# Expert rows gathered by six rounded products with the token rows split in two halves

## The reference

```python
def _moe(h, router, wg, wu, wd):
    logits = jnp.einsum('btd,de->bte', h.astype(jnp.float32), router.astype(jnp.float32))
    top_v, top_i = lax.top_k(logits, TOP_K)
    probs = jax.nn.softmax(top_v, axis=-1)
    gates = jnp.sum(jax.nn.one_hot(top_i, N_EXPERTS, dtype=jnp.float32) * probs[..., None], axis=-2)
    y = jnp.zeros_like(h)
    for e in range(N_EXPERTS):
        y = y + gates[..., e:e + 1].astype(h.dtype) * _swiglu(h, wg[e], wu[e], wd[e])
    return y
```

## Time and profile before

| | us |
|---|---|
| median of 3 runs | 1846.82 (1846.73 to 1847.57) |
| span of the profiled execution | 1844.9 |
| PE busy | 1671.4 (91%) |
| DVE busy | 1306.2 (71%) |
| ACT busy | 926.0 (50%) |
| GpSimd busy | 248.1 (13%) |

### The profile page before, as it was taken

One profiled execution on the slowest core, in us unless ns is written; L12 is line 12 of the kernel. 1 busy time (PEld: TensorE's weight loads), 2 busy tenths in 40 slices (PEclk: granted clock), 3 DMA queues, 4 the chain that ended last, 5 costly groups with the idle time before them and its releaser, 6 DMA issues.

```text
span 1844.9 us, 31414 instructions
## 1 busy us (share of the span) xinstructions
PE 1671.4 (91%) x11268; PEld 1512.7 (82%) x11268; DVE 1306.2 (71%) x1743; ACT 926.0 (50%) x1229; POOL 248.1 (13%) x132
## 2 busy tenths in 40 slices
PE   6948799989998966789988999999999999999997
PEld 6838786889987965777787979798998979798895
DVE  3798845454401397983536989889898989889896
ACT  4432102244301532211225868777787868778784
POOL 4645310000002553521000000000000000000000
PEclk8968889989999887898988999999999999999999
DMA  6522113265545342112334989989898989989892
GB/s 242 162 69 74 46 69 114 100 214 181 174 128 159 101 132 61 59 49 83 126 126 140 364 300 355 344 308 365 288 365 291 357 310 348 370 285 361 294 360 101
DMA packets 103843, 386.14 MB, mean 209 GB/s; under 512 B 11696, under 2 KB 11728, under 8 KB 103008
## 3 DMA queue, kind: packets, MB, share of 16 engines
q1 hardware_dynamic: 102096, 372.00, 57.1%
q0 software_dynamic: 1680, 13.20, 2.0%
HBM read 377.79 MB, written 7.37 MB: 209 GB/s over the span
## 4 chain that ended last, share of the span: by engine, by line
PE 76%; DVE 18%; ACT 2%; issue 2%; DMA 0%; POOL 0%; SPq 0%; DVEq 0%; ACTq 0%
PE psum L1163 52%; DVE c L816 8%; PE psum L1407 4%; PE psum L1441 3%; DVE qkv L842 2%; PE psum L1198 2%; PE psum L1379 2%; PE psum L1499 2%; PE psum L1381 2%; DVE hT L767 1%; PE psum L1332 1%; PE psum L1362 1%; PE psum L1267 1%; PE psum L1230 1%; PE psum L1206 1%
## 5 line engine op out<-in xcount | busy, mean ns | idle before, releaser
L1098 DVE TENSOR_TENSOR w_lo<-ring,w_hi 128x1024 fp32r<-128x1024 f32 x528 | 644.6, 1224 | 72.0 <-ACT w_hi L711 65.7
L711 ACT ACTIVATE w_hi<-ring 128x1024 fp32r<-128x1024 f32 x528 | 557.7, 1061 | 143.0 <-PE psum L1163 136.0
L1163 PE MATMUL psum<-w_hi,h_hi 128*96 128x256 f32 x1408 | 402.1, 286 | 5.5 <-DVE w_lo L1098 5.5
L1163 PE MATMUL psum<-w_hi,h_lo 128*96 128x256 f32 x1408 | 394.7, 280 | 0.0
L1163 PE MATMUL psum<-w_lo,h_hi 128*96 128x256 f32 x1408 | 393.7, 280 | 0.0
L1163 PE MATMUL psum<-hid_hi,w_hi 128*128 128x264 f32 x1024 | 305.6, 298 | 39.7 <-POOL w_lo L418 30.0
L1163 PE MATMUL psum<-hid_lo,w_hi 128*128 128x264 f32 x1024 | 299.8, 293 | 0.0
L1163 PE MATMUL psum<-hid_hi,w_lo 128*128 128x264 f32 x1024 | 298.9, 292 | 0.0
L1163 PEld LDWEIGHTS psum<-hid_hi,w_hi 128*128 128x128 f32 x1024 | 203.4, 199 | 45.7 <-POOL w_lo L418 30.9
L1163 PEld LDWEIGHTS psum<-w_hi,h_hi 128*96 128x96 f32 x1408 | 228.5, 162 | 8.7 <-DVE w_lo L1098 7.4
L418 POOL TENSOR_TENSOR w_lo<-ring,w_hi 128x1024 fp32r<-128x1024 f32 x68 | 167.3, 2468 | 477.8 <-ACT w_hi L531 477.8
(11 more groups left out here) (280 smaller groups left out, 2000.7 us busy)
## 6 DMA issues: line engine op xcount, KB each, us to landing
ring<-in_w_exp SPq DMA_DIRECT2D x528, 512.0 KB, 5.3
ring<-in_w_mixer SPq DMA_DIRECT2D x112, 512.0 KB, 3.6
ring<-in_w_ffn SPq DMA_DIRECT2D x66, 512.0 KB, 3.5
early<-in_s POOLq DMA_DIRECT2D x2, 2048.0 KB, 8.6
out_ss<-early POOLq DMA_DIRECT2D x2, 2048.0 KB, 6.9
xT<-in_xT SPq DMA_DIRECT2D x1, 1056.0 KB, 5.0
out_yT<-hT POOLq DMA_DIRECT2D x1, 1056.0 KB, 4.2
early<-in_dw_win POOLq DMA_DIRECT2D x2, 496.0 KB, 5.8
```

The source lines that it names most:

```text
L711: A(w_hi[:, (n_split + u) % SPLIT, :], ring[:, u % RING, :, :].rearrange("p k n -> p (k n)"), ACT.Copy).then_inc(hi_done, 1)
L1098: V.tensor_tensor(w_lo[:, (n_split + u) % SPLIT, :], ring[:, u % RING, :, :].rearrange("p k n -> p (k n)"), w_hi[:, (n_split + u) % SPLIT, ...
L1163: last = M(out, lhs[x], rhs[w], start=(start and n == 0), stop=(stop and n == 2))
```

## The change

`h_tok` becomes two tensors of the rounded type: `tok_hi`, which ACT writes at the old place with the same three copies, and `tok_lo`, which DVE writes over `early` with three subtractions of `tok_hi` from the PSUM banks. DVE waits for `state_out` before the first, since `early` must have left. `take` becomes rounded too, at its old place; ones and zeros are exact in it. Each product of the gather becomes two, one with each half. PE waits for the third `tok_lo` where it waited for the third `h_tok`.

```diff
+EARLY_AT, GS_AT, WORK_AT = 78464, 115968, 132864
...
-        h_tok = gs[:, :, :].rearrange("p k t -> p (k t)")[:, 0:3 * D].rearrange("p (m d) -> p m d", m=3)
+        tok_hi = nc.alloc_sbuf_tensor_at("tok_hi", [P, 3, D], F32R, offset=GS_AT)
+        tok_lo = nc.alloc_sbuf_tensor_at("tok_lo", [P, 3, D], F32R, offset=EARLY_AT)
+        take = nc.alloc_sbuf_tensor_at("take", [P, 3, CAP], F32R, offset=WORK_AT + 8 * U * P * 4)
...
-        take = work[:, 8, 0:3 * CAP].rearrange("p (m s) -> p m s", m=3)
...
-                        A(h_tok[:, m, :], psum[:, (0, 2, 6)[m]:(0, 2, 6)[m] + 2, :].rearrange("p b n -> p (b n)"), ACT.Copy).then_inc(h_tok_done, 1)
+                        A(tok_hi[:, m, :], psum[:, (0, 2, 6)[m]:(0, 2, 6)[m] + 2, :].rearrange("p b n -> p (b n)"), ACT.Copy).then_inc(h_tok_done, 1)
...
+                    def token_low(m):
+
+                        dve.wait_ge(h_tok_done, m + 1)
+                        V.tensor_tensor(tok_lo[:, m, :], psum[:, (0, 2, 6)[m]:(0, 2, 6)[m] + 2, :].rearrange("p b n -> p (b n)"), tok_hi[:, m, :], ALU.subtract).then_inc(tok_lo_done, 1)
...
                     settle(V.memset(scan[:, :, :], 0.0))
+                    dve.wait_ge(state_out, 16 * 6 * DEPTH)
+                    for m in range(3):
+                        token_low(m)
                     dve.wait_ge(ranks_mm, 1)
...
                             for m in range(3):
-                                last = M(psum[:, part, k % 4 * CAP:(k % 4 + 1) * CAP], h_tok[:, m, k * P:(k + 1) * P], take[:, m, :],
-                                         start=(m == 0), stop=(m == 2))
+                                for n, tok in enumerate((tok_hi, tok_lo)):
+                                    last = M(psum[:, part, k % 4 * CAP:(k % 4 + 1) * CAP], tok[:, m, k * P:(k + 1) * P], take[:, m, :],
+                                             start=(m == 0 and n == 0), stop=(m == 2 and n == 1))
                         last.then_inc(gather_mm, 1)
-                    pe.wait_ge(h_tok_done, 3)
+                    pe.wait_ge(tok_lo_done, 3)
```

More of the change, by code:

```diff
@@ L275, in build @@
         h_tok_done = sem("h_tok_done")
+        tok_lo_done = sem("tok_lo_done")
         chosen = sem("chosen")
```

## The result

The changed kernel takes **1853.1 us**, the median of 6 runs, beside 1847.16 for 6 runs of the kernel before: a ratio of 1.0037, with a 95% interval of 1.0024 to 1.0049. It is slower by 5.9 us; the forecast was slower by 4.1. The profiled execution took 1852.78 us with a span of 1851.0; the span before was 1844.9.

What follows compares the result with a forecast made beforehand. The experts' chain on PE bounds the kernel, rounded weight products holding 52% of the span. 0 + 0.6 + 1.2 + 1.3 + 1.0 = 4.1 us on 1846.8 gave 1850.9 us, range 1845.5 to 1865.

Steps and rivals of the forecast that it cites:

- gather in the job loop: Gather halves in the job loop: 24 loads of the same length before and after, so 0 us.
- DVE's subtractions: Three subtractions on DVE ahead of the copy of the ranks, mostly hidden by PE's rank products: +0.6 us.
- rows product: Rows product after the first half: begins at half clock, which rises 3.1 us into it: +1.2 us.
- second half: Second gather half ahead of the first job: takes 5.41 us at half clock instead of 4.14: +1.3 us.
- first weight products: First weight products of the first job: longer at half clock, losing 1.5 us instead of 0.5: +1.0 us.
- The mechanism: Ahead of the first job: the rounded half doesn't bring the clock back, slowing what follows; +3.5 us.
- forecast's own range: Whole kernel: 1849 to 1853.5 us, the top with 3.1 us of half clock in rows product and weights each.
- DVE's small instructions: Small DVE instructions writing the rounded take: possibly 0.1 us a job, 1 us in all; in the range, not the sum.
- The clock doesn't mind: Rival, ahead of the first job: clock rises in the rounded half as before, only DVE's 0.6 us left; 1847.4 us, chance 0.27.
- The clock falls in the job loop too: Rival, job-loop gathers: falls of 1.7 us in 8 of the 16 halves, 13.6 us more; 1865 us, chance 0.10.
- The narrow rounded product is slow: Rival, all gather halves: 0.05 us more per product, 1.2 us a half; 1869 us, chance 0.09.
- Rounded loads are fast: Rival, gather halves: a half shrinks to 1.2 us, 18.8 us gained in eight jobs; 1828.6 us, chance 0.09.

Runs made afterwards that it cites:

- e3: Changed kernel with the 16 loop halves plain (high half alone), the two ahead of the loop rounded, plus one unused half; 1855.03 us, ratio 1.0039.
- e2: Changed kernel with the two halves ahead of the loop plain (high half alone), the loop rounded, plus one unused half; 1849.46 us, ratio 1.0013.
- e4: Changed kernel plus unused 512-column products where PE was idle, five after the rank products and three after the rows product; 1846.62 us, ratio 0.9995.
- e1: Changed kernel with the three subtractions kept but the gather plain, on unrounded rows and an unrounded take; 1847.65 us, ratio 0.9999.
- e5: Kernel before the change plus unused 512-column products, five after the rank products and three after the rows product; 1843.92 us, ratio 0.9977.
- e7: Kernel before the change plus fewer unused 512-column products, four after the rank products and two after the rows product; 1843.19 us, ratio 0.9983.
- e8: Changed kernel with 48 instead of 96 moving columns in every gather product, still 24 products a half; 1864.31 us, ratio 1.0078.
- e6: Changed kernel with the low half's products left out of the gather, 12 products and loads a half instead of 24; 1834.57 us, ratio 0.9929.

## Why the prediction was nearly right

By its own steps, with the places measured in the two profiles (before from the earlier trace rows, after from the fences of the first section):

| step of the sum | forecast, us | measured, us | how |
|---|---|---|---|
| gather in the job loop | 0 | -0.2 | first job-end half to the last load: 734.5 before, 734.3 after; e3 less its unused half stands at the change |
| DVE's subtractions | +0.6 | +0.5 | router's start to the copy of the ranks: 16.69, 17.22 |
| rows product | +1.2 | +1.5 | first half's start to the rows product's end: 8.28, 9.77 |
| second half | +1.3 | +1.2 | second half's start to the first weights: 3.85, 5.15, less 0.1 in DVE's copies |
| first weight products | +1.0 | +1.6 | first weights to the job's end: 96.29, 97.86 |
| sum | +4.1 | +4.6 | |
| ahead of the router | 0 | +1.5 | its start: 956.34, 957.86 |

**The mechanism was right.** The rounded half did not bring the clock back (0.50 from its start to the end), e2 and e3 put the whole loss into the two halves ahead of the loop, and e4 gives the time back by work that does nothing but keep PE busy, though the rounded half still loses the clock there.

**The term that was mis-sized** is how long dense work needs to bring the clock back. I took about 3 us for both places, after the transposes. The rows product saw half clock for about 3.7 us (from 984.89 to 988.6, by the 0.85 in 988 to 990), and the weight products for about 4.5 (from 997.73 in the chain to 1002.2, by the 0.94 in 1002 to 1004). So the rows product lost 0.3 more than the sum said and the weights 0.6 more. The result is within the forecast's own range, but near its end of 1853.5, which held one fall in the loop and 1 us for DVE's small instructions. Neither came: the job loop kept 1.00, and from the copy of the ranks to the first half the small instructions take 4.69 us in both traces. That the range reached so far is luck. Below 1850.5 the forecast would have counted as no change; the result lies above that, and its interval begins at 0.24%.

**What the sum can't hold.** The 1.5 us ahead of the router lie where the change has no instruction. I take it as the scatter of one execution, not as a part of the loss: e2, with the subtractions and the rounded loop, starts its router at 956.06 and e3 at 957.40, and they differ by nothing ahead of it. Counted from the router's start, by the chains, the traces are free of it:

| trace | router's start | first job's end begins | between | from there to the end |
|---|---|---|---|---|
| before | 956.34 | 1089.06 | 132.7 | 755.8 |
| the change | 957.86 | 1095.39 | 137.5 | 755.6 |
| e1, plain gather | 956.99 | 1089.82 | 132.8 | 756.0 |
| e2, plain ahead of the loop | 956.06 | 1088.59 | 132.5 | 757.8 (unused half) |
| e3, plain in the loop | 957.40 | 1094.92 | 137.5 | 758.2 (unused half) |
| e4, the change filled | 964.76 | 1097.03 | 132.3 | 755.7 |
| e5, before filled | 962.30 | 1090.88 | 128.6 | 755.8 |
| e7, before filled less | 956.91 | 1085.49 | 128.6 | 755.8 |

So the loss behind the router is 4.8 us ahead of the first job's end and nothing after it. About 1 us between these traces and the medians' 5.9 (5.6 between e2 and e3) is within what the intervals allow; it stays open.

**What would show it**, as the prediction put it: the pieces of 2.7 us at each job's end, the copy of the ranks 0.5 us later, the clock at 0.50 through the first half and again in the second, all came. The weight products began 39.67 us behind the router's start, where they had begun 36.43 behind it: 3.2 later; the forecast's 996 was 3.2 later than 992.8.

**The rivals.**

- *The clock doesn't mind* fell: it gave 1847.4, but the clock did not rise in the rounded half, and the change takes 1853.1. With the plain gather put back (e1) that time is met, 1847.65.
- *The clock falls in the job loop too* fell for 96 columns: 1.00 in every stretch from 1020. It was a fair rival, though: e8 shows the mechanism at 48 columns. That its 1864.3 us is nearly the rival's 1865 is chance, since the rival counted eight falls of 1.7 us and e8's trace has six of unequal length.
- *The narrow rounded product is slow* fell: 2.62 to 2.71 us a half in the loop.
- *Rounded loads are fast* fell: 192 ns. The time that it gave, 1828.6, rested on a step under 0.10 us. e6, which halves the loads instead, shows that the arithmetic was about right in kind: 1.35 us saved by the half ahead of the scatter, less by the one behind it, since DVE's `w_lo` ends last there.

Two rules of the Trainium skill were weighed. By the four passes of true fp32 (the Trainium skill, "FP8 and Floating Point Precision", TensorE Precision Notes), the change should have won in the gather, if passes set the time. The trace doesn't count passes (a plain product has two records), but they do not set the time of products so narrow: e8 halves the columns and e6 halves the loads, and only the loads matter. The fast weight load (the Trainium skill, "TensorE: Matmul & The Clock Gate", Weight-path perf modes) is not to be seen for the rounded type: 24 rounded loads take what 24 plain ones take.

The Trainium skill ("TensorE: Matmul & The Clock Gate", Why this matters for your kernels) advises against long idle gaps between bursts of products, because the clock falls back. This is what e5 and e7 carry out, and the measured 3.3 and 4.0 us bear it out for plain products. In e4, with the gaps closed to 0.61 us and less, a rounded half of narrow products still lost the clock.

## What to carry to other kernels

Count loads before columns: with 8 to 96 moving columns, a product's record here cost the same 0.11 us with its load, and fewer passes bought nothing while the number of loads stayed. A change that lightens what TensorE does in a stretch of gaps and hand-overs can slow down the dense work behind it through the clock, as it did here; read the granted clock behind the stretch, not only the stretch itself. Where such gaps can't be closed, a few products that nobody needs may be worth their place: six of them, put where TensorE was idle, took some 4 us off the kernel before.

## What the runs showed of the hardware that was not expected

- A busy TensorE can lose its full clock. In e4, a rounded half of 24 products that began at 1.00 ran 2.9 us (986.82 to 989.76) with 0.61 us of idle time ahead of it and almost none behind, and the dense product behind it took 4.40 us instead of 2.84. The plain half in the same place kept 1.00 (e5, and e7 with 1.26 us of idle time ahead of it), and in the job loop, between dense products of many us, the rounded half kept it too. What the loop has that e4's stretch lacks was not tried.
- Less work can be slower: with half the columns the kernel took 1864.3 us instead of 1853.1, and at the first job's end the scatter behind the half took 7.02 us instead of 3.63.
- How long dense work took to bring the clock back differed from place to place, with PE busy throughout: 3.1 us in transposes of 128 columns, 3.7 in the rows product, 4.5 in the weight products. The kind of work does not settle it, since in e4 the same weight products had it back after 3.3 us (999.87 to 1003.2, by the 0.71 in 1002 to 1004), and before the change after 1.0 (992.77 to about 993.8). Why they differ stays open.
